# Issuing the z tiles of the scan whole, in four places of a group, instead of in quarters between the steps

## What is computed

```python
proj = hn @ w_in
z, xbc, dt_raw = jnp.split(proj, [SSD_INNER, SSD_INNER + SSD_XBC], axis=-1)
...
y = bidir_scan(qc, kb, v_f, v_b, log_a[:, :, 0].reshape(grp), log_a[:, :, 1].reshape(grp))
y = y + xh * d_skip...
y = y.reshape(bsz, s, SSD_INNER) * jax.nn.silu(z.astype(f32))
...  # rms norm over each of the 4 groups, then @ w_out
```

## Time and profile before

| | |
|---|---|
| median of 3 runs | 2037.21 us (2033.24 to 2037.58) |
| the profiled execution | 2037.06 us |
| its span in the trace | 2035.1 us |
| granted TensorE clock, mean over the span | 0.954 of 2.4 GHz |
| TensorE (PE) matmuls busy | 1844.2 us |
| VectorE (DVE) busy | 1222.3 us |
| ScalarE (ACT) busy | 752.0 us |
| GpSimd (POOL) busy | 188.6 us |
| the scan in the span | about 1267 to 1544 us |

### The profile page before, as it was taken

One profiled execution on the slowest core, in us unless ns is written; L12 is line 12 of the kernel. 1 busy time (PEld: TensorE's weight loads), 2 busy tenths in 40 slices (PEclk: granted clock), 3 DMA queues, 4 the chain that ended last, 5 costly groups with the idle time before them and its releaser, 6 DMA issues.

```text
span 2035.1 us, 20666 instructions
## 1 busy us (share of the span) xinstructions
PE 1844.2 (91%) x8186; PEld 1421.4 (70%) x8186; DVE 1222.3 (60%) x1647; ACT 752.0 (37%) x1278; POOL 188.6 (9%) x212
## 2 busy tenths in 40 slices
PE   7998989998968889999996999889879969999996
PEld 5885557885346668888884777557657848888885
DVE  4435463435678548877335599566566357877523
ACT  4236432212133334443323344445454225544321
POOL 0301200002041001111000000012012001111000
PEclk9999989998968889999997999899999979999998
DMA  5331002331010222333331222011001203323331
GB/s 192 104 95 41 1 31 90 117 100 56 0 27 21 77 72 94 94 103 91 99 100 38 98 83 94 23 40 32 25 28 53 95 29 118 101 94 97 93 94 68
DMA packets 42751, 147.86 MB, mean 73 GB/s; under 512 B 5152, under 2 KB 6304, under 8 KB 42528
## 3 DMA queue, kind: packets, MB, share of 16 engines
q1 hardware_dynamic: 39168, 138.43, 21.4%
q10 hardware_dynamic: 3488, 8.12, 1.2%
HBM read 144.44 MB, written 2.10 MB: 72 GB/s over the span
## 4 chain that ended last, share of the span: by engine, by line
PE 79%; DVE 14%; ACT 4%; issue 2%; POOL 1%; ACTq 0%; DMA 0%; DVEq 0%; POOLq 0%
PE bank L309 22%; PE bank L310 21%; PE bank L311 21%; DVE cv L1375 2%; PE bank L509 2%; DVE w_lo L278 2%; PE bank L1474 1%; PE bank L927 1%; PE bank L516 1%; DVE x L447 1%; PE bank L1456 1%; PE bank L935 1%; PE bank L1447 1%; PE bank L1465 1%; PE bank L1436 1%
## 5 line engine op out<-in xcount | busy, mean ns | idle before, releaser
L309 PE MATMUL bank<-a_hi,w_hi 128*128 128x512 f32 x1504 | 608.3, 404 | 70.2 <-DVE w_lo L278 33.9
L310 PE MATMUL bank<-a_lo,w_hi 128*128 128x512 f32 x1504 | 592.6, 394 | 0.0
L311 PE MATMUL bank<-a_hi,w_lo 128*128 128x512 f32 x1504 | 591.9, 394 | 0.0
L278 DVE TENSOR_TENSOR w_lo<-raw,w_hi 128x1024 fp32r<-128x1024 f32 (+1 forms) x264 | 354.9, 1348 | 290.5 <-ACT w_hi L271 290.1
L271 ACT ACTIVATE w_hi<-raw 128x1024 fp32r<-128x1024 f32 (+1 forms) x264 | 273.3, 1041 | 374.3 <-DMA raw<-in_w_in 169.2
L309 PEld LDWEIGHTS bank<-a_hi,w_hi 128*128 128x128 f32 x1504 | 287.0, 191 | 142.1 <-issue 59.8
L310 PEld LDWEIGHTS bank<-a_lo,w_hi 128*128 128x128 f32 x1504 | 287.0, 191 | 64.8 <-issue 6.7
L311 PEld LDWEIGHTS bank<-a_hi,w_lo 128*128 128x128 f32 x1504 | 286.6, 191 | 61.3
L836 ACT ACTIVATE u<-bank,par 128x512 f32<-128x512 f32 x88 | 68.7, 780 | 223.8 <-DVE bank L474 223.8
L309 PE MATMUL bank<-g_hi,w_hi 128*128 128x512 f32 x352 | 136.9, 389 | 0.0
L310 PE MATMUL bank<-g_lo,w_hi 128*128 128x512 f32 x352 | 136.9, 389 | 0.0
(11 more groups left out here) (347 smaller groups left out, 2203.8 us busy)
## 6 DMA issues: line engine op xcount, KB each, us to landing
raw<-in_w_up SPq DMA_DIRECT2D x88, 512.0 KB, 3.4
raw<-in_w_in SPq DMA_DIRECT2D x52, 512.0 KB, 3.4
raw<-in_w_out SPq DMA_DIRECT2D x32, 512.0 KB, 3.5
raw<-in_w_down SPq DMA_DIRECT2D x32, 512.0 KB, 3.5
raw<-in_w_xbc SPq DMA_DIRECT2D x24, 512.0 KB, 3.4
raw<-in_w_z SPq DMA_DIRECT2D x16, 512.0 KB, 3.4
raw<-in_w_down SPq DMA_DIRECT2D x16, 384.0 KB, 3.1
x<-in_xT ACTq DMA_DIRECT2D x4, 512.0 KB, 6.9
```

Of the source, the lines that this page charges most:

```text
L278: nc.vector.tensor_tensor(w_lo[:, q % RING, 0:w], raw[:, q % RING, 0:w], w_hi[:, q % RING, 0:w].bitcast(F32), ALU.subtract).then_inc(lo_do ...
L309: nc.tensor.matmul(out, wh, rhs_hi[:, k, :], start=k == 0, stop=False)
L310: nc.tensor.matmul(out, wh, rhs_lo[:, k, :], start=False, stop=False)
L311: return nc.tensor.matmul(out, wl, rhs_hi[:, k, :], start=False, stop=stop)
```

## The change

In each group, z tile 4g+2 is issued whole after `states(g, 0)`, z tile 4g+3 whole after the first two spreads and ahead of `norm_sum`, z tile 4g+4 whole in step m = 0 and z tile 4g+5 whole in step m = 4 of the second stage. Nothing else changes: the same instructions, other places on TensorE.

```diff
+        def whole_z(t):
+            for q in range(4):
+                part_z(t, q)
+
         for g in range(SG):
             begin(g)
-            part_z(4 * g + 2, 0)
             states(g, 0)
-            part_z(4 * g + 2, 1)
+            whole_z(4 * g + 2)
             between(g, 0)
-            part_z(4 * g + 2, 2)
             states(g, 1)
-            part_z(4 * g + 2, 3)
             between(g, 1)
-            part_z(4 * g + 3, 0)
             states(g, 2)
-            part_z(4 * g + 3, 1)
             between(g, 2)
             spread(g, 0)
             spread(g, 1)
-            part_z(4 * g + 3, 2)
+            whole_z(4 * g + 3)
             if g:
                 norm_sum(g - 1)
-            part_z(4 * g + 3, 3)
             for m in range(8):
                 if m < 7:
                     spread(g, 2 * m + 2)
                     spread(g, 2 * m + 3)
                 if m % 2 == 0:
                     carried(g, m // 2)
-                if g + 1 < SG:
-                    part_z(4 * g + 4 + m // 4, m % 4)
+                if m % 4 == 0 and g + 1 < SG:
+                    whole_z(4 * g + 4 + m // 4)
                 inside(g, m)
```

## The result

The changed kernel takes 2069.44 us (median of 4 runs, 2061.45 to 2073.4) against 2035.22 us (median of 4 runs of the kernel before): a ratio of 1.0163, 95% interval 1.0129 to 1.0197. The forecast was 2065.6 us, 28.5 us more. The profiled execution took 2070.03 us, its span 2068.2 us, 33.1 us over the span of before.

The account below looks back on a forecast made before the run. TensorE fills the first stage (23.74 of 24.40 us), z quarters covering the recurrence's waits for VectorE. Order 15.3, second-stage holes 6.0 and clock 7.2 sum to 28.5 us more: 2065.6 us, range 2052 to 2074.

Parts of the forecast that it names:

- Order of the first stage: First stage of all groups: thirteen z quarters of delay, 17.9 us, less 3 x 0.86 for norm_sum; +15.3 us.
- the quarter in front was free: Group 0, first stage: TensorE idles 0.43 us before states(0) anyway, so the z quarter ahead of it cost nothing.
- The clock behind the hole: Behind the new 4.8 us TensorE hole, first stage: half clock costs 1.8 us in each of four groups, +7.2 us.
- Second stage: Groups 0 to 2: inside(0) comes late, ScalarE runs out of spreads, new holes cost 2.0 us a group, +6.0 us.
- A: Rival: the clock stays up in the new first-stage hole; 21.3 us more, 2058.4 us; 12%.
- B: Rival: ScalarE catches up and the second stage costs nothing; 2059.6 us; 8%.
- C: Rival: second stage wins nothing back (12.5 us), clock costs 2.5 a hole; 37.8 us more, 2074.9 us; 8%.
- D: Rival: the place of z doesn't matter, a transfer or ScalarE paces the group; 2037 us; 3%.
- E: Rival: changing between f32 passes and z matmuls costs TensorE time; at 1.16 a visit saves 48.7 us, 2016.9 us; 3%.

Follow-up runs that it names:

- e3_fill: The changed kernel plus 16 unused matmuls before each group's last between and 7 ahead of states(0) in group 0; 2057.51 us, ratio 1.0115.
- e4_tile2: The kernel before with only z tile 4g+2 whole, after states(0), all other tiles in quarters; 2040.36 us, ratio 1.0033.
- e7_whole_wait: The changed kernel with z tile 4g+4 whole behind norm_sum, ahead of step m = 0 instead of inside it; 2059.75 us, ratio 1.0117.
- e1_first: The kernel before with whole z tiles in the first stage only, quarters kept in the second; 2061.29 us, ratio 1.0135.
- e2_second: The kernel before with whole z tiles in the second stage only, quarters kept in the first; 2042.92 us, ratio 1.0044.
- e12_copy: Kernel before with whole tiles in the second stage only, weight copy behind n = 10 instead of n = 8 in groups 0 to 2; 2044.35 us.

## Why the prediction was right, and where it was short

*Order of the first stage* (forecast 15.3 us). Right. `states(1)` came 1.32 us later from `begin` in groups 1 to 3 (forecast 1.3). The chain from it to the last "between" was 10.06 us before and after, so VectorE does set it, and the hole was 4.6 us (forecast 4.8). That chain holds a weight split and take_z (1.22 and 0.68 us in the changed kernel), which the recurrence doesn't need; whether the hole shrinks with these moved behind fed(2) was not tried. Behind the last "between" `e3_fill`, with the clock kept up, has 8.4 us; the kernel before plus two quarters less norm_sum gives 6.57 + 2.77 - 0.86 = 8.5. The first stages took 25.7 us more in all, of which 10.8 are clock, so order took 14.9.

*Group 0, "the quarter in front was free".* This step was incomplete. As work it was free, but it kept TensorE busy. Without it the wait for vtl grew to 1.82 us, behind one of 1.86 us, and the clock fell at 1274.4 (last row of the first table): 1.7 us that the sum didn't have. It doesn't happen in every execution. The same instructions with the same two waits cost it in the traces of the changed kernel, `e4_tile2` and `e7_whole_wait` and not in that of `e1_first`. So the 1.7 us belong to the profiled execution, and that `e3_fill` doesn't have them shows nothing by itself. The timeline of the changed kernel, group 0:

```profile
1270.96 1.15 PE L1420 MATMUL bank<-cst,xbc 128*128 128x128 f32 x8 [1.86 <-ACT xtok L1579]
1273.93 3.26 PE L1436 MATMUL bank<-vtl,btok 128*128 128x512 f32 x4 [1.82 <-DVE vtl L1654]
```

and the pair of `states(0)` in `e1_first`, at the full clock:

```profile
1272.95 1.95 PE L1436 MATMUL bank<-vtl,btok 128*128 128x512 f32 x4 [1.82 <-DVE vtl L1654]
```

*The clock behind the hole* (forecast 7.2 us, bounds 0 and 10). Right in mechanism, and the term was sized low: 9.1 us. I had taken 1.8 a hole by the nearest gap; two groups paid 1.6 and 1.7, the other two 2.8 and 3.0, because there the granted clock came back only some 6 us after work had begun again. The rows had both kinds (3.4 us in the earlier trace rows, 5.0 in the earlier trace rows), and I had gone by the first. In `e1_first` all four holes were of the dear kind, 2.6 to 3.0 us each, 11.4 in all, above my upper bound of 10.

*Second stage* (forecast 6.0 us). Right in kind, low in size: 7.4 us in the trace of the changed kernel; `e2_second` alone has 7.7 us in its trace and 9 us (6 to 12) by its runs. The hole of step 4 was 1.05 us (forecast 1.2) and is the weight copy's, as `e12_copy` shows. The term that I had mis-sized is the last step: inside(7) waits 1.03 us for the last weighing, not 0.2, because step 7 lost its quarter.

So 15.3 + 6.0 + 7.2 became 14.9 + 7.4 + 9.1 + 1.7 = 33.1. What the prediction had wanted to see in the profile is there: the hole put down to VectorE's hst, the granted clock of 0.50 behind it, take_z late by 6.1, 4.8 and 6.0 us in groups 1 to 3 (3.2 plus the clock) and by 8.8 in group 0. In group 1 inside(0) comes 4.2 us later after the first Exp (forecast about 4), inside(7) 2.9 us (forecast about 2, short by the wait of step 7).

The largest term, order, was right, and the misses of the others all go the same way, so nothing cancelled by luck. But the clock's share is that of one execution: a hole of 4.6 us cost anything from 1.6 to 3.0 us, so four of them could have cost 6.4 to 12.

*The rivals.* A (the clock stays up) falls by the tables above. `e3_fill` is what A would have looked like: +21.3 was forecast for it, +23.4 measured. The Trainium skill, TensorE: Matmul & The Clock Gate, section "Loop structure matters more than you think", which A leaned on, is right that gaps cost the clock (0.50 behind every hole of 4.6 us here). But wholeness is not what kept it here: the quarters were what filled the gaps. B (ScalarE catches up) falls by `e2_second`. Of C the clock's price was near the truth, the 12.5 us in the second stage were not. D falls by every run. E (changing between f32 and z costs TensorE time) would have made `e2_second` and `e1_first` faster, and both were slower. A whole tile takes 1358.93 - 1353.44 = 5.49 us, four quarters' worth of matmuls to within 0.05 us (the tile's start taken as 1.72 us behind the pair's), and a pair with no z behind it takes 1360.64 - 1358.93 = 1.71 us, against the 1.72 of one that z follows.

## What to carry to other kernels

Work that depends on nothing is worth most where its engine would otherwise wait, cut as small as the waits are; moved in one piece behind the wait, it is paid for once as order and once more as clock. Before moving such filler, list the waits it covers, each with its length, since here the clock fell behind every hole of 3.3 and 4.6 us that whole tiles made, and not behind those of 1.8 us in groups 1 to 3. The largest wait (here 6.6 us for ScalarE's tables) is the place for a whole tile, and once it is filled, ask which engine's queue ends next: here it was VectorE's, with work of the group before.

## What was not expected of the hardware

The same hole costs a different amount each time. In one execution of the changed kernel four holes of 4.6 us were followed by about 3.4 or 6 us of work at half clock, 1.6 to 3.0 us of loss each. The traces show what goes with the one and the other. Twelve holes of this length stand in the traces of the changed kernel, `e1_first` and `e7_whole_wait`. In three the granted clock fell within 0.4 us of the start of the pair behind the hole and stayed at 0.50 for 3.4 us. In nine it had fallen 0.6 to 1.4 us before that start, still within the hole, and stayed at 0.50 for 6.8 to 7.0 us. Why it falls early in one and late in the other was not tried.

That the runs scatter (2061.45 to 2073.4 us) because of these holes isn't shown. The code ahead of the scan is the same in all fourteen traces, and the first `begin` comes anywhere from 1260.2 to 1269.9 us.

Adding matmuls made two kernels faster: 88 of them took 5.5 us (3 to 8) off the kernel before, 71 took some 10 us off the changed one.

The clock fell also where no single hole is long. In group 0 two waits of 1.86 and 1.82 us with 1.15 us of transposes between them were enough in three of four traces (not in `e1_first`); in `e4_tile2` a hole of 1.8 us left it up in groups 1 to 3 and not in group 0; in `e12_copy` it fell at the `begin` of group 1, behind waits of 1.03 and 0.85 us.
